# Convolution channels shared out anew: TensorE 3 to 2, VectorE 5 to 4, ScalarE with GpSimd 0 to 2

## The reference, cut to what matters

```
def conformer_conv(h, w_pw1, b_pw1, w_dw, b_dw, ln_g, ln_b, w_pw2, b_pw2):
    a, gt = jnp.split(h @ w_pw1 + b_pw1, 2, axis=-1)
    z = a * jax.nn.sigmoid(gt)
    z = lax.conv_general_dilated(            # 31 taps back in time, each channel by itself
        z, w_dw[:, None, :], window_strides=(1,), padding=[(CONV_WIDTH - 1, 0)],
        dimension_numbers=('NWC', 'WIO', 'NWC'), feature_group_count=D_MODEL) + b_dw
    z = jax.nn.silu(layernorm(z, ln_g, ln_b))
    return z @ w_pw2 + b_pw2
```

## Time and profile before

| | |
|---|---|
| median of 3 runs | 3040.37 us (3039.09 to 3042.96) |
| the profiled execution's own time | 3033.97 us |
| its span | 3032.2 us |
| busy: PE, DVE, ACT, POOL | 94%, 67%, 38%, 3% |
| granted TensorE clock, mean | 0.966 |
| first products and convolution | about 2009 to 2247 us of the span |

### The profile page before, as it was taken

The page is one execution under the profiler, slowest core; times in us unless marked ns, Lnnn a source line. Parts: engine busy times, 40 slices in busy tenths (PEclk is TensorE's granted clock), DMA queues, the critical chain, the costliest instruction groups (busy, mean ns, idle before and its releaser), DMA issues.

```text
span 3032.2 us, 39599 instructions
## 1 busy us (share of the span) xinstructions
PE 2841.1 (94%) x15451; PEld 2339.6 (77%) x15451; DVE 2033.7 (67%) x3470; ACT 1163.3 (38%) x1969; POOL 82.3 (3%) x152
## 2 busy tenths in 40 slices
PE   3999999688999998899999999989989999999999
PEld 3878885466888887678888888868757788888887
DVE  5444317768445556558777778779985877777875
ACT  3234227534225555434333334431134433333444
POOL 1000000210130000000000000000000000000000
PEclk7999999898998999799999999999989999999999
DMA  8110200024100000223333274311101333335632
GB/s 310 29 32 22 63 28 10 5 85 126 42 18 1 1 1 1 91 97 111 112 111 111 84 282 142 97 48 47 36 16 63 105 112 111 111 111 194 217 96 102
DMA packets 185700, 256.28 MB, mean 85 GB/s; under 512 B 29575, under 2 KB 138539, under 8 KB 181035
## 3 DMA queue, kind: packets, MB, share of 16 engines
q1 hardware_dynamic: 181520, 232.45, 23.3%
q10 hardware_dynamic: 3995, 21.30, 1.7%
HBM read 186.62 MB, written 67.11 MB: 84 GB/s over the span
## 4 chain that ended last, share of the span: by engine, by line
PE 67%; DVE 8%; ACT 1%; issue 1%; DMA 0%; DVEq 0%; ACTq 0%
PE ps L1567 27%; PE ps L1575 14%; PE ps L1522 10%; PE ps L1470 4%; PE ps L1380 3%; PE ps L1452 2%; PE ps L1434 2%; PE ps L1631 2%; PE ps L1122 1%; PE ps L1682 1%; PE ps L1001 1%; PE ps L1668 0%; DVE ht L2836 0%; PE ps L1358 0%; PE ps L1428 0%
## 5 line engine op out<-in xcount | busy, mean ns | idle before, releaser
L1567 PE MATMUL ps<-x_ops,w_ring 128*128 128x512 f32 x3696 | 840.3, 389 | 6.3 <-ACT even_rows L2185 3.2
L1567 PEld LDWEIGHTS ps<-x_ops,w_ring 128*128 128x128 f32 x3696 | 693.1, 188 | 151.6 <-issue 7.9
L1575 PE MATMUL ps<-a_ring,w_ring 128*128 128x512 f32 x1848 | 419.7, 389 | 0.0
L1575 PEld LDWEIGHTS ps<-a_ring,w_ring 128*128 128x128 f32 x1848 | 346.7, 188 | 72.6 <-DVE w_ring L2925 0.7
L1522 PE MATMUL ps<-h_high,ring_parts 128*128 128x512 f32 x1024 | 320.6, 394 | 18.0 <-DVE h_low L2409 9.3
L2127 ACT ACTIVATE w_ring<-ring 128x512 fp32r<-128x512 f32 x230 | 144.2, 629 | 300.6 <-PE ps L1567 284.8
L1522 PEld LDWEIGHTS ps<-h_high,ring_parts 128*128 128x128 f32 x1024 | 193.5, 190 | 63.7 <-issue 13.5
L2418 DVE TENSOR_TENSOR ring_parts<-ring,ring_parts 128x1024 fp32r<-128x1024 f32 (+2 forms) x77 | 91.7, 1192 | 210.1 <-ACT ring_parts L1769 209.5
L1522 PE MATMUL ps<-h_low,ring_parts 128*128 128x512 f32 x512 | 200.7, 392 | 0.0
L2925 DVE TENSOR_TENSOR w_ring<-ring,w_ring 128x512 fp32r<-128x512 f32 x230 | 157.6, 685 | 38.8 <-ACT w_ring L2127 38.8
L1769 ACT ACTIVATE ring_parts<-ring 128x1024 fp32r<-128x1024 f32 (+2 forms) x77 | 76.0, 989 | 275.7 <-PE ps L1522 177.2
(11 more groups left out here) (476 smaller groups left out, 4637.2 us busy)
## 6 DMA issues: line engine op xcount, KB each, us to landing
a_raw<-act_kept SPq DMA_DIRECT2D x70, 512.0 KB, 3.8
act_kept<-even_rows SPq DMA_DIRECT2D x12, 1536.0 KB, 5.1
act_kept<-odd_rows SPq DMA_DIRECT2D x10, 1536.0 KB, 5.1
ring<-in_ffn_w_gate_dram SPq DMA_DIRECT2D x12, 1024.0 KB, 5.8
ring<-in_ffn_w_up_dram SPq DMA_DIRECT2D x12, 1024.0 KB, 6.0
ring<-in_conv_w_pw_dram SPq DMA_DIRECT2D x24, 512.0 KB, 3.9
late<-in_ffn_w_gate_dram SPq DMA_DIRECT2D x10, 1024.0 KB, 5.8
late<-in_ffn_w_up_dram SPq DMA_DIRECT2D x10, 1024.0 KB, 6.1
```

What stands on the lines that cost most here:

```text
L1567: last = mm(o, w_ring[:, i % 4, wp_, P * k:P * k + P], x_ops[:, X_OP[p], rp_, k, :], start=p in "176" and k == 0 and p_ == 0, stop=k == 3 ...
L1575: last = mm(bank(OUT_BANK[DOWN_GROUP[p] + c_]), w_ring[:, (A_UNITS + b) % 4, wp_, P * c_:P * c_ + P], a_ring[:, b % 4, rp_, :], start=p in ...
```

## The change

Chunks 6 and 7 stay on TensorE (`PE_CONV`), 0, 2, 4 and 5 go to VectorE (`DVE_CONV`), and 1 and 3 to ScalarE with GpSimd (`POOL_CONV`).

- *ScalarE and GpSimd.* For each of its chunks GpSimd makes the two differences, ScalarE multiplies shifted planes by a tap, two products of 512 columns into one of three buffers (`pool_made`), and GpSimd adds the buffer to the running sum in SBUF (`pool_acc`), 1024 columns at once. ScalarE does 4 of the 24 steps of a chunk in each half period (`products_at`), from the third on, and waits for a buffer to be free (`taps_added`); GpSimd waits for the products (`taps_made`). The three buffers lie where ScalarE later puts `quarter_sums`, so it waits for GpSimd's last step before it copies the first bank.
- *VectorE.* The running sums of its chunks 0, 2 and 4 lie in PSUM, in banks 4 and 5; those of chunk 5 lie in SBUF, because TensorE uses the banks by then. The order of the steps stays as it was; the fifth chunk and the sums over chunks fall away.
- *TensorE.* It convolves two chunks and starts when three of VectorE's are done. The sums over channels are four pairs of matmuls, with `pool_sum` among them, in which GpSimd has added five chunks.
- Six semaphores of the first block are merged into three, with the same waits.

The diff, without the renamed semaphores:

```diff
--- before.py
+++ after.py
@@ -232,8 +232,12 @@
         zp = part(8192, (KC, 2, HALF))
         zc = zp[:, :, :, 0:S // 2]
         flat_sc = sc[:, :, :].rearrange("p a b -> p (a b)")
-        tap_tiles = flat_sc[:, 0:3 * CONV_W * 32].rearrange("p (c t n) -> p c t n", c=3, t=CONV_W)
-        stacked = flat_sc[:, 3 * CONV_W * 32:3 * CONV_W * 32 + 32]
+        tap_tiles = flat_sc[:, 0:2 * CONV_W * 32].rearrange("p (c t n) -> p c t n", c=2, t=CONV_W)
+        stacked = flat_sc[:, 1984:2016]
+        pool_acc = flat_sc[:, 2016:3040].rearrange("p (two m) -> p two m", two=2)
+        pool_later = flat_sc[:, 3040:3040 + HALF - 1]
+        pool_made = [part(17648 + 1024 * i, (2, 512)) for i in range(3)]
+        pool_sum = sc[:, 2, :]
         quarter_sums = [part(17648 + 512 * i, (512,)) for i in range(7)] + [dists[:, 0:512]]
         sg = part(16624, (S,))
         later = part(21616, (HALF - 1,))
...
@@ -584,7 +587,14 @@
 
         N_PAR = 21
         N_PW = 0
-        PE_CONV = (KC - 3, KC - 2, KC - 1)
+        PE_CONV = (KC - 2, KC - 1)
+        DVE_CONV = (0, 2, 4, 5)
+        POOL_CONV = (1, 3)
+
+        def added_at(count):
+
+            return 26 * (count // 24) + 2 + count % 24 + (count % 24 >= 8)
+
...
@@ -1641,6 +1651,7 @@
                 last.then_inc(s.fold_out, 1)
 
             pe.wait_ge(s.taps_ok, 1)
+            pe.wait_ge(s.zc_ok, 3)
             for c_, n in enumerate(PE_CONV):
                 pe.wait_ge(s.up_free, N_PW + n + 2)
                 if c_:
@@ -1652,15 +1663,18 @@
                 tap_sums(c_, 0)
                 fold(c_, 1)
                 fold(c_, 0)
+            pe.wait_ge(s.zc_ok_pe, 2)
+            for half in range(2):
+                mm(bank(2 + half), ones[:, :], zc[:, PE_CONV[0], half, :], start=True, stop=False)
+            pe.wait_ge(s.zc_sum, 1)
+            for half in range(2):
+                mm(bank(2 + half), ones[:, :], pool_sum[:, 512 * half:512 * half + 512], start=False, stop=False)
+            pe.wait_ge(s.zc_ok, 4)
+            for half in range(2):
+                mm(bank(2 + half), ones[:, :], zc[:, DVE_CONV[3], half, :], start=False, stop=False)
             pe.wait_ge(s.zc_ok_pe, 4)
             for half in range(2):
-                mm(bank(2 + half), ones[:, :], zc[:, KC - 2, half, :], start=True, stop=False)
-            pe.wait_ge(s.zc_ok_pe, 6)
-            for half in range(2):
-                mm(bank(2 + half), ones[:, :], zc[:, KC - 1, half, :], start=False, stop=False)
-            pe.wait_ge(s.zc_sum, KC - 3)
-            for half in range(2):
-                last = mm(bank(2 + half), ones[:, :], sc[:, 3, 512 * half:512 * half + 512], start=False, stop=True)
+                last = mm(bank(2 + half), ones[:, :], zc[:, PE_CONV[1], half, :], start=False, stop=True)
             last.then_inc(s.mean_done, 1)
...
@@ -2266,15 +2280,56 @@
                 norm_high(4, k)
                 if k == 0:
                     high(T_PW1 + 1)
+            tap = lambda t, n: cols[:, V_WDW + 8 * t + n:V_WDW + 8 * t + n + 1]
+
+            def tap_products(turn, step):
+
+                n, count = POOL_CONV[turn], 24 * turn + step
+                even, odd = zp[:, n, 0, :], zp[:, n, 1, :]
+                if step == 0:
+                    a.wait_ge(s.up_free, N_PW + n + 2)
+                    if turn:
+                        a.wait_ge(s.taps_added, 26 * turn)
+                    f(pool_acc[:, 0, :], odd[:, 0:512], ACT.Identity, bias=cols[:, V_BDW + n:V_BDW + n + 1],
+                      scale=sum_taps[:, 0, n:n + 1])
+                    f(pool_acc[:, 1, :], odd[:, 1:513], ACT.Copy, scale=sum_taps[:, 1, n:n + 1]).then_inc(s.taps_made, 1)
+                    return
+                made = pool_made[count % 3]
+                a.wait_ge(s.taps_added, 26 * turn + 2)
+                if count > 3:
+                    a.wait_ge(s.taps_added, added_at(count - 3))
+                if step < 8:
+                    f(made[:, 0, :], odd[:, 2 * step:2 * step + 512], ACT.Copy, scale=sum_taps[:, 2 * step, n:n + 1])
+                    ins = f(made[:, 1, :], odd[:, 2 * step + 1:2 * step + 513], ACT.Copy,
+                            scale=sum_taps[:, 2 * step + 1, n:n + 1])
+                elif step == 8:
+                    ins = f(made[:, 0, :], even[:, 0:512], ACT.Copy, scale=tap(0, n))
+                else:
+                    m = step - 9
+                    f(made[:, 0, :], even[:, m + 1:m + 513], ACT.Copy, scale=tap(2 * m + 2, n))
+                    ins = f(made[:, 1, :], pool_later[:, m:m + 512], ACT.Copy, scale=tap(2 * m + 1, n))
+                ins.then_inc(s.taps_made, 1)
+
+            def products_at(half_period):
+
+                if 3 <= half_period < 15:
+                    turn, part_ = (half_period - 3) // 6, (half_period - 3) % 6
+                    for step in range(4 * part_, 4 * part_ + 4):
+                        tap_products(turn, step)
+
+            a.wait_ge(s.taps_ok, 1)
             for n in range(KC):
                 a.wait_ge(s.gate_out, N_PW + n + 1)
                 if n < KC - 1:
                     high(T_PW1 + 2 * n + 2)
                 a.wait_ge(s.up_free, N_PW + n + 1)
                 f(sg, bank(0, 2), ACT.Sigmoid, bias=cols[:, V_BPW1 + 8 + n:V_BPW1 + 9 + n]).then_inc(s.gate_free, 1)
+                products_at(2 * n)
                 if n < KC - 1:
                     a.wait_ge(s.up_out, N_PW + n + 1)
                     high(T_PW1 + 2 * n + 3)
+                    products_at(2 * n + 1)
+            a.wait_ge(s.taps_added, added_at(47))
...
@@ -3298,7 +3353,7 @@
 
                 even, odd = zp[:, n, 0, :], zp[:, n, 1, :]
                 out = zc[:, n]
-                acc, other_ = sc[:, 3, 0:512], sc[:, 3, 512:1024]
+                acc, other_ = (sc[:, 3, 512:1024], out[:, 1, :]) if n == DVE_CONV[3] else (bank(4), bank(5))
                 for t in steps:
                     if t == 0:
                         chain(differences(n, later))
@@ -3330,21 +3385,13 @@
             low(T_PW1 + 2)
             between(0); convolve(0, range(0, 8)); low(T_PW1 + 4); convolve(0, range(8, 18))
             between(1); convolve(0, range(18, 25)); low(T_PW1 + 6); convolve(0, range(25, STEPS))
-            between(2); convolve(1, range(0, 9)); low(T_PW1 + 8); convolve(1, range(9, 18))
-            between(3); convolve(1, range(18, 24)); low(T_PW1 + 10); convolve(1, range(24, STEPS))
-            between(4); convolve(2, range(0, 8)); low(T_PW1 + 12); convolve(2, range(8, 17))
-            between(5); convolve(2, range(17, 24)); low(T_PW1 + 14); convolve(2, range(24, STEPS))
-            between(6); convolve(3, range(0, 18))
-            between(7); convolve(3, range(18, STEPS))
-            convolve(4, range(0, STEPS))
+            between(2); convolve(2, range(0, 9)); low(T_PW1 + 8); convolve(2, range(9, 18))
+            between(3); convolve(2, range(18, 24)); low(T_PW1 + 10); convolve(2, range(24, STEPS))
+            between(4); convolve(4, range(0, 8)); low(T_PW1 + 12); convolve(4, range(8, 17))
+            between(5); convolve(4, range(17, 24)); low(T_PW1 + 14); convolve(4, range(24, STEPS))
+            between(6); convolve(5, range(0, 18))
+            between(7); convolve(5, range(18, STEPS))
             planes = lambda row: row.rearrange("p (two m) -> p two m", two=2)
-            v.wait_ge(s.zc_ok, KC - 3)
-            tt(planes(sc[:, 3, :]), zc[:, 0], zc[:, 1], add).then_inc(s.zc_sum, 1)
-            for k in range(2, KC - 2):
-                if k in PE_CONV:
-                    v.wait_ge(s.zc_ok_pe, 2)
-                v.wait_ge(s.zc_sum, k - 1)
-                tt(planes(sc[:, 3, :]), planes(sc[:, 3, :]), zc[:, k], add).then_inc(s.zc_sum, 1)
             v.wait_ge(s.mean_done, 1)
 
             def squares_added(p_):
@@ -3477,6 +3524,41 @@
             stage(g, "mixer_attended")
             stage(g, "x_3")
             g.memset(zp[:, :, :, 0:HALF - 512], 0.0).then_inc(s.pad_ok, 1)
+            added = [0]
+
+            def taken(o, x, y, op):
+                added[0] += 1
+                g.tensor_tensor(o, x, y, op).then_inc(s.taps_added, 1)
+                g.wait_ge(s.taps_added, added[0])
+
+            def convolve(turn, n):
+
+                even, odd = zp[:, n, 0, :], zp[:, n, 1, :]
+                g.wait_ge(s.up_free, N_PW + n + 2)
+                taken(pool_later, even[:, 1:], odd[:, 0:HALF - 1], ALU.subtract)
+                taken(even, even, odd, ALU.subtract)
+                g.wait_ge(s.taps_made, 24 * turn + 1)
+                for step in range(1, 24):
+                    made = pool_made[(24 * turn + step) % 3]
+                    g.wait_ge(s.taps_made, 24 * turn + step + 1)
+                    if step < 8:
+                        taken(pool_acc, pool_acc, made, ALU.add)
+                    elif step == 8:
+                        taken(pool_acc[:, 1, :], pool_acc[:, 0, :], pool_acc[:, 1, :], ALU.add)
```

(51 more changed lines are left out.)

## The result

The changed kernel takes 3049.36 us (median of 6 runs, 3046.76 to 3052.51) against 3040.22 us for the kernel before (6 runs, 3035.2 to 3044.59): a ratio of 1.0029, 95% interval 1.0017 to 1.0042. It is slower by 9.1 us; forecast were 8.3 (3048.7 us).

What follows compares the result with a forecast made beforehand. TensorE was taken as the bounding chain, VectorE beside it with hardly any room. Tap sums 23.6 us late, -17.7 for the channel and +2.4 for the clock gave +8.3 on 3040.4: 3048.7 us, range 3026 to 3057.

Steps and rivals of the forecast that it cites:

- The part with one answer: TensorE loses a channel, 19.47 us, and gets a fourth pair of column sums, 1.73 us: 17.7 us less.
- the port: VectorE and GpSimd take turns when both read two SBUF operands; a VectorE split took 3.18 us instead of 1.22.
- Rival (b): GpSimd's additions cost 1.89 us and ScalarE's last block paces it; gated(7) 17.9 us late, 3043.0 us; chance 0.17.
- Step 1: Beside the first products, waiting splits and differences make VectorE's last split 15.7 us late and TensorE's products end 9.8 late.
- Step 2: VectorE's last chunk alternates with seven GpSimd instructions, waiting 14.1 us; TensorE stands idle 14 us for gated(7).
- Step 3: TensorE's tap sums after the wait for gated(7) start at a slow clock: 2.4 us lost.
- The sum: Second half of tap sums starts 23.6 us late; with -17.7 and +2.4 that is +8.3 us, 3048.7 us.
- (a): VectorE's waits for GpSimd's SBUF use cost nothing and gated(7) is in time: -17.7, 3022.7 us; chance 0.12.
- middle case: Splits wait but GpSimd is done before VectorE's last chunk: -17.7 + 9.8, 3032.5 us; chance 0.14.
- (c): VectorE's back-to-back steps keep the port, GpSimd starves and its second chunk ends late: 3051.6 us; chance 0.08.
- (d): VectorE's running sums in PSUM are dear: 141 steps cost 9 us more, up to 3057.8 us; chance 0.03.
- (e): ScalarE, held by GpSimd, feeds TensorE late in the products; all of Step 1 doubles, 3058 us; chance 0.04.

Runs made afterwards that it cites:

- two sums: Changed kernel with gated(7) after 3 steps of VectorE's last chunk, and two running sums that GpSimd fills in turn instead of adding in place: 3028.09 us.
- thin additions: Changed kernel with GpSimd's additions on 4 columns of each plane instead of 512, column sums reading chunk 1 instead of GpSimd's sum: 3020.82 us.
- steps moved: Changed kernel with gated(7) ahead of the whole last VectorE chunk and convolution steps moved behind the splits: 3030.52 us.
- shifted sum: Changed kernel with GpSimd's running sum and the differences behind it moved by 4 words: 3053.18 us.
- early gated(7): Changed kernel with VectorE running gated(7) after 3 steps of its last chunk instead of 18: 3035.61 us.

## Why the prediction was right, and where its steps were not

**The part with one answer.** 17.7 us; 17.76 with the port free. Right.

**ScalarE and GpSimd.** ScalarE's products took 718 and 709 ns (0.72 assumed). GpSimd's additions took 2.42 us alone (2.39 assumed), 2.7 in turns with VectorE. The reason given, a distance of 16 words, is wrong; that the price fitted was luck, or at best owed to the earlier trace rows having more dear cases than cheap ones. Rival (b) was the price of 1.89. Even two sums give only 2.00 and 2.40.

**Step 1.** The mechanism is shown by the kernels with thin additions (gone) and with steps moved (absorbed). The sizes:

| | predicted | measured |
|---|---|---|
| last split late by | 15.7 us | 17.4 us |
| products' end late by | 9.8 us | 13.5 us |

The last split ended at 2187.97, 166.8 us after the products' start, against 149.4 (2166.89 - 2017.52). The ten splits beside GpSimd took 2.36 us on average, so each waited 1.14 us (1.08 predicted); an eleventh, which began 0.26 us before GpSimd's first instruction, took its ordinary 1.23. The differences cost 1.75 + 2.82 and 2.88 + 2.78 instead of 0.7 each (timeline of VectorE):

```profile
2134.18 3.04 DVE L2473 TENSOR_TENSOR ring_parts<-ring,ring_parts 128x1024 fp32r<-128x1024 f32 x1
2137.14 2.88 DVE L3349 TENSOR_TENSOR big<-big 128x526 f32<-128x526 f32 x1
2140.06 2.78 DVE L3350 TENSOR_TENSOR big<-big 128x527 f32<-128x527 f32 x1
```

Of the 3.7 us by which the products' end missed, the late split is 1.7, and 1.9 are the last product itself: it took 12.78 us (2188.12 to 2200.90), where 10.9 were put. That is the term that was missing, the clock inside the products; I counted one for the wait at gated(7) only. In all, TensorE's idle times in the products sum to 8.65 us, and 4.9 of the 13.5 are products that took longer. 3.5 of these are the slow clock behind two stalls, as these stretches show (busy time of each engine with its count, then the granted clock; the first begins with the product after 3.63 us of idle time, the second follows it at once, the third begins with the one after 2.47 us):

```profile
core 0: us, PE busy (x) PEld busy (x) DVE busy (x) ACT busy (x) POOL busy (x), PEclk, DMA share, GB/s
2137.30:2142.30 5.00, 4.94 (x15) 3.93 (x16) 4.96 (x2) 2.31 (x4) 4.89 (x2) 0.66 0.40 110
2142.30:2147.00 4.70, 4.70 (x22) 3.88 (x21) 4.49 (x7) 1.34 (x2) 4.58 (x2) 1.00 0.00 0
2188.00:2193.00 5.00, 4.88 (x14) 3.88 (x15) 4.89 (x4) 4.54 (x8) 3.73 (x2) 0.66 0.17 51
```

15 and 14 matmuls in 5 us where the full clock (2.4 GHz, granted 1.00) makes some 23: about two thirds of each stretch was granted the lower level (1.2 GHz). The two products took 12.76 and 12.78 us from their first matmul to their last one's end, against 11.04 for the last product before the change: 1.7 us lost behind each. The remaining 1.4 us lie around the shorter stalls, and there the granted clock was 1.00, so they are not the clock; what they are I did not test. This trace had only told of stalls of 5 us, and I left out what shorter ones do.

**Step 2.** Predicted: gated(7) at 2213.4 to 2215.4, TensorE idle for 14 us. Measured, less the 3.64 us by which the products started later: 2216.9 to 2218.9, idle for 13.14. From the last split's end to gated(7)'s start it was 32.6 us, 15.7 more than before (14.1 predicted, for seven instructions of GpSimd in between). Timelines of VectorE and GpSimd:

```profile
2189.37 2.49 DVE L3360 TENSOR_SCALAR sc<-big,cols 128x512 f32<-128x512 f32 x1
2191.90 25.84 DVE L3362 SCALAR_TENSOR_TENSOR sc<-big,sc 128x512 f32<-128x512 f32 x15
```

```profile
2189.19 7.75 POOL L3531 TENSOR_TENSOR sc<-sc,big 128x1024 f32<-128x1024 f32 x3 [2.30 <-ACT big L2310]
...
2208.22 2.68 POOL L3561 TENSOR_TENSOR sc<-sc,big 128x1024 f32<-128x1024 f32 x1
```

VectorE's 15 steps take 25.84 us instead of 11.8 (15 x 0.79), and become quick again once GpSimd's last addition has ended, at 2210.90. It was eight instructions that still stood in the way, and 2.7 us for each pair: 8 x 2.0 = 16, near the measured 15.7. With gated(7) moved ahead of the steps the wait was gone, as step 2 says.

Why eight were left is not what step 2 says. It had GpSimd 7 us behind when the last split ends. In fact GpSimd had nothing to do at that moment: from 2186.89 to 2189.19 it waited for ScalarE, whose last four steps stand behind the last sigmoid, and that waited for gated(6) (timeline of ScalarE):

```profile
2186.43 1.11 ACT L2326 ACTIVATE big<-ps,cols 128x1024 f32<-128x1024 f32 x1 [5.56 <-DVE big L3342]
```

gated(6) ended 165.2 us after the products' start, against 148.3 before: VectorE's delay holds up the pair's last block, which then stands in VectorE's way. Its 4 additions and the 4 of the sums make the eight. That is the pacing that rival (b) described for its cheaper price. Step 2's count (seven) was near the mark for another reason than the one given, which is luck; no run moved that block, so what it is worth is open.

**Step 3.** 2.4 us predicted; the 248 matmuls behind the wait took 10.36 us against 8.13 without one, 2.2. Right. (Of the two idle times that the term was read from, only the 5.07 us stood before such products; behind the 4.87 us came 1-column matmuls.)

**The sum.** The stage came out at -17.7 + 27.1 + 2.2 = +11.6 us, where 27.1 is the lateness of the second half of tap sums (201.4 after the products' start, 174.3 before). Predicted were 23.6, so it was 3.5 us short: 1.7 of the last split (step 1) and 1.8 between it and gated(7)'s start (step 2: 30.8 us predicted, 32.6 measured). The slow clock in the products is not among them, because TensorE, come later to its tap sums, waits that much less for gated(7). Once that wait is gone, the clock of the last product counts. The medians differ by 9.1 us and not by 11.6; a profile is one execution, and this 2.5 us lies within what runs of one kernel differ by. The kernel with the shifted sum, with the same stage of 246.32 us, came out 13.4 us above the kernel before. That the time came out within 0.7 us of the forecast is in part luck: the stage itself was 3.3 us further off.

**The rivals.** (a), the port decides nothing: refuted (thin additions 3020.82 us, changed kernel 3049.36). Its middle case, only the splits count, is what the early gated(7) makes of the kernel: 3032.5 us worked out, 3035.61 measured; the tap sums began 11.8 us late instead of 9.8, and 1.6 of the 2.0 between are the last split's (17.3 us late against 15.7). (b) fell with the price, though its pacing by ScalarE's last block is what happened. (c), starvation: GpSimd did not starve; it went in between any two of VectorE's steps. (d), dear PSUM sums: 756 against 752 ns in one run, in line with the earlier trace rows. The 62 cycles that the Trainium skill, page "VectorE: DVE Perf Modes", section "The TRN2 errata — SBUF-src ops pay a fixed extra latency per instruction", gives for PSUM sources are in neither, and the measurement decides. (e), ScalarE feeds TensorE late: TensorE waited for splits, and ScalarE's waits for buffers (10.9 us in 13 pieces, 2.3 at most) reached none of them.

## What to carry to other kernels

Before you give GpSimd two-operand work in SBUF, list VectorE's instructions that read two operands from SBUF in the same stretch, and price each at half an instruction of GpSimd if it comes alone and at a whole one if it comes in a row; then ask which of them somebody waits for. Move the running sums of VectorE into PSUM where banks are free (74 us here), and in its queue put what TensorE waits for ahead of what only has to be done some time (3049.36 to 3035.61 us here, for two lines). Work that waits for the delayed engine is delayed with it, and can come back to stand in its way, as the last four steps of ScalarE and GpSimd did here. And a short stall of TensorE can cost more than its length: behind 3.6 us of idle time the next product took 1.4 to 2.9 us more in the five traces that have such a stall, behind 2.25 to 2.47 us 1.7 more in three traces. In three traces a stall of 1.87 to 2.60 us cost 0.1 us or nothing, with the granted clock at 1.00 behind it. So its price is not fixed by its length.

## What the runs showed of the hardware

- An instruction of VectorE with one data operand from SBUF also takes turns, where it writes to SBUF. The first product of a chunk, L3360, took 582 ns into SBUF with the port free and 2493 beside GpSimd in the changed kernel (2480 to 2800 in five other traces), but 814 ns in both where it wrote to PSUM. (Details of that line, duration ns min/median/max, in the kernel with thin additions and in the changed one:)

```profile
L3360 DVE TENSOR_SCALAR sc<-big,cols x1: 582/582/582, 2173.8 to 2173.8; 128x512 f32<-128x512 f32 x1
```

```profile
L3360 DVE TENSOR_SCALAR sc<-big,cols x1: 2493/2493/2493, 2189.4 to 2189.4; 128x512 f32<-128x512 f32 x1
```

  That it is the faster of the two forms when alone fits the Trainium skill, page "SBUF — State Buffer", section "SBUF: two separate sides", by which VectorE takes the shared port pair for an instruction in a 2-port mode or with two SBUF inputs, and whoever starts first keeps it for the whole instruction. No run here shows the mode itself. On the second part the runs agree in the main: in turns a pair took 2.78 us, not much less than 2.41 + 0.75 = 3.16, so only some 0.4 us of it lie beside the other.
- The two engines alternate strictly, one for one, also where a step of VectorE is a third of GpSimd's (seven additions in 19.46 us in the kernel with all sums in SBUF). Neither starves.
- GpSimd's addition of 1024 columns took 1.89, 2.00 or 2.40 us alone, and each value came back: 1.89 six times in the trace before the change, 2.00 or 2.01 fourteen times with two sums, the third mostly between 2.38 and 2.43. Neither a multiple of 16 words between its inputs (moved by 4 words: 2.41) nor writing in place explains which.
